# Attention in a two-layer trunk: value products turned, weights normalised ahead of their transposes

## The reference, cut to what matters

```
first layer, for each query block of 128:
  p_cmp = masked_softmax(q . k_cmp * scale)       # 15 compressed keys
  p_sel = masked_softmax(q . k_sel * scale)       # with 256 tokens all blocks are selected
  p_win = masked_softmax(q . k_win * scale)       # the window covers all tokens, causal
  o = gate0 * p_cmp @ v_cmp + gate1 * p_sel @ v_sel + gate2 * p_win @ v_win
  return o @ w_out
second layer:
  p = masked_softmax(q . k * scale); o = p @ v; return o @ w_out
masked_softmax(s) = exp(s - max) / max(sum(exp(s - max)), 1e-30)
```

## Time and profile before

| | |
|---|---|
| median of 3 runs | 763.71 us (763.39 to 764.23) |
| profiled execution | 763.77 us |
| its span | 762.0 us |
| PE busy | 717.5 us (94%) |
| DVE busy | 518.1 us (68%) |
| ACT busy | 374.0 us (49%) |
| POOL busy | 273.0 us (36%) |

### The profile page before, as it was taken

The page is one execution under the profiler, slowest core; times in us unless marked ns, Lnnn a source line. Parts: engine busy times, 40 slices in busy tenths (PEclk is TensorE's granted clock), DMA queues, the critical chain, the costliest instruction groups (busy, mean ns, idle before and its releaser), DMA issues. The chain is left out here.

```text
span 762.0 us, 11217 instructions
## 1 busy us (share of the span) xinstructions
PE 717.5 (94%) x4085; PEld 581.2 (76%) x4085; DVE 518.1 (68%) x940; ACT 374.0 (49%) x696; POOL 273.0 (36%) x261
## 2 busy tenths in 40 slices
PE   4799999889999999999999889989999999999997
PEld 2577768678687888878788777868688888878886
DVE  3357687898466796977656887987567885554544
ACT  2255555576336444444432367776356444444431
POOL 7021211000103998979969641520106960000000
PEclk9999999999999999999999999999999999999999
DMA  8997994030563888896866546801846965654521
GB/s 288 355 371 219 359 353 149 1 112 2 189 197 112 262 286 279 254 298 202 288 242 208 156 161 182 312 12 58 283 158 188 284 215 170 187 185 181 171 106 55
DMA packets 93742, 154.05 MB, mean 202 GB/s; under 512 B 6235, under 2 KB 68320, under 8 KB 93696
## 3 DMA queue, kind: packets, MB, share of 16 engines
q1 hardware_dynamic: 80768, 111.24, 44.1%
q0 software_dynamic: 12928, 42.20, 17.4%
HBM read 151.32 MB, written 1.05 MB: 200 GB/s over the span
## 5 line engine op out<-in xcount | busy, mean ns | idle before, releaser
L1079 DVE TENSOR_TENSOR w_lo<-raw,w_hi 128x1024 fp32r<-128x1024 f32 (+3 forms) x198 | 286.3, 1460 | 146.3 <-ACT w_hi L734 145.8
L734 ACT ACTIVATE w_hi<-raw 128x1024 fp32r<-128x1024 f32 (+3 forms) x198 | 201.4, 1024 | 268.8 <-PE lin L1724 244.6
L1722 PE MATMUL lin<-w_hi,st_hi 128*128 128x512 f32 (+2 forms) x568 | 227.9, 401 | 0.1
L1724 PE MATMUL lin<-w_hi,st_lo 128*128 128x512 f32 (+2 forms) x568 | 219.4, 386 | 0.0
L1723 PE MATMUL lin<-w_lo,st_hi 128*128 128x512 f32 (+2 forms) x568 | 218.8, 385 | 0.0
L602 POOL DMA_DIRECT2D ada_ring<-in_ada_w_dram x80 | 45.2, 566 | 258.5 <-PE sc L1845 221.0
L1722 PEld LDWEIGHTS lin<-w_hi,st_hi 128*128 128x128 f32 x568 | 107.5, 189 | 29.1 <-issue 8.5
L1724 PEld LDWEIGHTS lin<-w_hi,st_lo 128*128 128x128 f32 x568 | 107.4, 189 | 21.3
L1723 PEld LDWEIGHTS lin<-w_lo,st_hi 128*128 128x128 f32 x568 | 107.6, 189 | 19.0 <-issue 0.7
L681 POOL TENSOR_TENSOR pool_acc<-pool_acc,ada_ring 128x1024 f32<-128x1024 f32 x40 | 115.6, 2889 | 3.3
L1722 PE MATMUL lin<-w_hi,hid_hi 128*128 128x512 f32 x176 | 69.7, 396 | 0.4 <-DVE hid L1251 0.4
(11 more groups left out here) (262 smaller groups left out, 889.1 us busy)
## 6 DMA issues: line engine op xcount, KB each, us to landing
raw<-in_ffn_w_in_dram SPq DMA_DIRECT2D x88, 512.0 KB, 5.0
ada_ring<-in_ada_w_dram POOLq DMA_DIRECT2D x80, 512.0 KB, 4.8
raw<-in_ffn_w_out_dram SPq DMA_DIRECT2D x22, 1024.0 KB, 5.3
raw<-in_nsa_w_in_dram SPq DMA_DIRECT2D x10, 1024.0 KB, 12.6
ada_first<-in_ada_w_dram SPq DMA_DIRECT2D x8, 1024.0 KB, 13.1
raw<-in_nsa_cmp_w_dram SPq DMA_DIRECT2D x4, 1024.0 KB, 11.5
raw<-in_nsa_w_out_dram SPq DMA_DIRECT2D x4, 1024.0 KB, 9.5
raw<-in_mla_w_out_dram SPq DMA_DIRECT2D x4, 1024.0 KB, 8.2
```

The lines of the kernel that those rows point to most:

```text
L734: nc.scalar.activation(part_of(w_hi, s), raw_part(s), ACT.Copy).then_inc(hi_ready, 1)
L1079: nc.vector.tensor_tensor(part_of(w_lo, s), raw_part(s), part_of(w_hi, s).bitcast(F32), ALU.subtract).then_inc(lo_ready, 1)
L1722: nc.tensor.matmul(bank, a_h, w_h, start=first, stop=False)
L1724: return nc.tensor.matmul(bank, a_l, w_h, start=False, stop=last)
```

## The change

- Items are handled in pairs, 16 in the first layer and 8 in the second. The loops of all three engines go over pairs. A pair's scores, its transposes (two pairs later) and its value products (three pairs later) are together.
- The value products have v stationary (64 wide) and the turned weights moving; the result is the output turned (channels on partitions, tokens in columns), the two heads of a pair in the lower and upper half of the partitions. Eight items (first layer: both branches of four heads) or four (second layer) gather in one bank, so the branches of the first layer are added up by the bank. The compressed branch's product opens each bank of the first layer.
- For that the weights have to be normalised and gated before. VectorE does that: per pair, `factors` (sum times the stored 1 + exp(-gate), reciprocal) and `normalise` (four multiplications in place, 128 and 256 columns for each head). The reciprocal of the gates is gone. The compressed weights are multiplied in one operation per token tile.
- The output is evicted from its bank directly as stationary halves (`group_high` on ScalarE, `group_low` on VectorE), four groups in each layer. The transposes of the output, their evictions, and the adding into `o0` are gone.
- Of four copies to `prob_t` ScalarE now does three, VectorE one. There are six buffers for the weights and four for the turned ones.
- The banks of scores and outputs are chosen anew per layer; 12 and 6 idle products stand ahead of the two groups of compressed transposes.
- TensorE's scores wait for the maxima of two pairs before, not for exponentials.

The diff, its core (constants, declarations and bookkeeping are left out):

```diff
+T_P0 = _batches(2 * H, "act", "dve", "act", "act")
+ST_O0 = _evictions(G)
+T_P1 = _batches(H, "act", "dve", "act", "act")
+ST_O1 = _evictions(H // R)
+        score0, summed0 = [sc[0], sc[1], lin[0], lin[1]], [lin[2], lin[3]]
+        score1, summed1 = [sc[0], sc[1], lin[2], lin[3]], [lin[0], lin[1]]
 # ScalarE, attention
+                for q in range(n_pairs + 3):
+                    before(q)
+                    if q < n_pairs:
+                        for j in range(2):
+                            n = 2 * q + j
+                            act.wait_ge(maxed, item0 + n + 1)
...
+                    if q >= group + 3 and (q - 3) % group == 0 and k < groups - 1:
+                        group_high(k)
+                    for n in range(2 * q - 4, 2 * q - 2):
+                        if 0 <= n < 2 * n_pairs and TP_EMPTIED[tp0 + n] == "act":
...
 # VectorE
+            def compressed_weights(t):
+                dve.wait_ge(cmp_exped, t + 1)
+                link(nc.vector.tensor_reduce(cf, tfull[:, t, :].rearrange("p (h c) -> p h c", c=CP), X, ALU.add))
+                link(nc.vector.scalar_tensor_tensor(cf4, cf4, TINY, gates_by_pair[:, t, :, :, :, 0], ALU.max,
+                                                    ALU.mult))
+                nc.vector.reciprocal(cf, cf).then_inc(cmp_summed, 1)
+            def factors(p, item0, gated):
+                dve.wait_ge(exped, item0 + 2 * p + 2)
...
+                if gated:
+                    link(nc.vector.scalar_tensor_tensor(cf, total, TINY, gates_of(p), ALU.max, ALU.mult))
+                else:
+                    link(nc.vector.tensor_scalar(cf, total, TINY, None, ALU.max))
+                nc.vector.reciprocal(cf, cf).then_inc(factored, 1)
+            def normalise(p, pair0, prob_b):
+                dve.wait_ge(factored, pair0 + p + 1)
+                for j in range(2):
+                    buf = prob_b[(2 * p + j) % 6]
+                    for t in range(T):
+                        cols = buf[:, t * P:t * P + (t + 1) * P]
+                        ins = nc.vector.tensor_scalar(cols, cols, coef[:, p % 3, 2 * t + j:2 * t + j + 1], None, ALU.mult)
+                ins.then_inc(normed, 1)
 # VectorE, attention: scores of pair q, behind(q) = factors and normalise of pair q - 1, copies of pair q - 2, group_low
-            def nsa_step(k): ...
-            def nsa_add(k): ...
-            def output_low(batch0): ...
-            def mla_step(k): ...
 # TensorE, attention
+                def values(p):
+                    k, m = divmod(p, group)
+                    bank = banks[k % 2]
+                    if m == 0:
+                        if k >= 2:
+                            pe.wait_ge(st_ready, st0 + k - 1)
+                        bank_begun[0] = group_start(k, bank)
+                    pe.wait_ge(*emptied(tp0 + 2 * p))
+                    pe.wait_ge(*emptied(tp0 + 2 * p + 1))
+                    c0 = (p % 2) * S
+                    for t in range(T):
+                        for u in range(2):
+                            n = 2 * p + u
+                            half = slice(DH * u, DH * u + DH)
+                            ins = nc.tensor.matmul(bank[half, c0 + t * P:c0 + S], v_of(n, t),
+                                                   prob_tb[n % 4][:, t * S:t * P + S],
...
+                for q in range(n_pairs + 3):
+                    before(q)
+                    if q < n_pairs:
+                        scores(q)
+                    if 2 <= q < n_pairs + 2:
+                        pe.wait_ge(normed, pair0 + q - 1)
+                        for n in (2 * q - 4, 2 * q - 3):
+                            transposes(tp0 + n, [prob_b[n % 6][:, j * P:(j + 1) * P] for j in range(3)])
+                    if q >= 3:
+                        values(q - 3)
...
-            pe.wait_ge(o_steps, 8)
-            for m in range(2):
-                o_batch(o0)(T_O0, m)
-            unit(U_OUT0, OUT0, FOUR, 512, stationary, st_wait(T_O0, o_batch(o0)), EACH)
+            unit(U_OUT0, OUT0, FOUR, 512, stationary, output_wait(ST_O0), EACH)
```

## The result

Median 770.44 us (768.41 to 771.68, 4 runs) against 763.85 (763.39 to 764.23, 4 runs): ratio 1.0083, 95% interval 1.0057 to 1.0109. The direction was the forecast's; the size, 6.6 us for 2.8, was not, and it stands just outside 762.0 to 770.0. The profiled execution took 771.68 (span 769.9), 7.9 over that of the kernel before.

A forecast was written before the change was run, and what follows sets the result against it. TensorE was busy 94%, VectorE nearly as full in attention; after the change VectorE's queue was to bound attention. 763.8 + 1.9 + 5.9 - 3.1 - 2.2 = 766.3, with 0.2 left out by the sum 766.5 us; range 762.0 to 770.0.

The forecast's parts named there:

- Part 1: TensorE's value products in attention: a pair's two heads run side by side, 0.86 us a pair, bounds 0.7 and 1.5.
- Rival (c): Value products: the two column halves don't overlap, a pair costs 1.5 us, 771.5 us in all; chance 0.07.
- Part 2: VectorE's normalisation in attention: four multiplications in place cost 0.91 us a pair, bounds 0.68 and 1.2.
- Part 3: First layer's attention: VectorE's queue sums to 54.9 us and attention ends at 191.7, +1.9 us.
- the term of the low evictions: VectorE in the first layer's attention: three low evictions wait for ScalarE's high half, 3 x 0.6 = 1.8 us.
- Rival (a): Attention: TensorE sets the pace and is faster; 761.0 us with cheaper multiplications, 750 without VectorE waits; chance 0.14.
- Part 4: Second layer's attention: VectorE's queue sums to 34.9 us and attention ends at 536.9, +5.9 us.
- busy over 90%: Sign for both attention stages: VectorE busy over 90% between the first scores and the stage's end.
- Part 5: Boundaries behind attention: output transposes gone, the modulation chunk's transfer late next; -3.1 and -2.2 us.
- Part 6: Items priced at nothing: 18 idle products (2.0 us) and ScalarE's extra copies lie in waits or idle time.
- from the boundary on everything moves alike: Code behind the attention boundaries: POOL and SP not in the way, everything shifts together, priced at nothing.
- Rival (b): Second layer's attention: holes in TensorE's work cost it the clock, up to 1.8 us a fall, 767 to 769.5; chance 0.18.

The follow-up runs named there:

- e4: Changed kernel with one single-column multiplication in place of each pair's four normalising ones, output not the reference's; 0.9990, 763.29 us.
- e2: Kernel before with nmax grown from 32 to 48 bytes, moving the tiles behind it by 32 bytes; 1.0007.
- e5: Changed kernel with nmax made 96 bytes, putting the tiles behind it on multiples of 128 bytes; 1.0073.
- e1: Changed kernel with nmax made 64 bytes, which left all tiles at the same places, so a repeat; 1.0081.
- e3: Changed kernel with many idle products (18, 25, 10, 17) in four of TensorE's holes; 1.0155.
- e6: Changed kernel with fewer idle products (8, 10, 4, 7) in the same four TensorE holes as e3; 1.0065.
- e9: e5 with the second layer's last root sums moved to the start of its attention on VectorE; 1.0027.
- e13: Changed kernel with GpSimd leaving out its last modulation chunk, output not the reference's; 1.0061.
- e14: Changed kernel as it is, run again; 1.0087.
- e15: Changed kernel with tiles on multiples of 128 bytes, e6's idle products and GpSimd's last chunk left out; 1.0009.
- e17: Changed kernel with tiles on multiples of 128 bytes and e6's idle products, nothing left out; 1.0034.
- e16: Kernel before with GpSimd leaving out its last modulation chunk, output not the reference's; 0.9965.
- e18: Kernel before with tiles on multiples of 128 bytes, a repeat of e12; 0.9983.
- e7: e4 with ScalarE's copies of transposed weights put ahead of the exponentials of the pair two later; 0.9934.
- e10: e9 with ScalarE doing all copies of transposed weights, these and the group copies ahead of the exponentials; 0.9938.
- e12: Kernel before with nmax made 96 bytes, putting its tiles on multiples of 128 bytes; 0.9972.
- e8: e5 with the 256-column multiplications on GpSimd and the second layer's last root sums at its attention's start; 0.9995.

## Why the prediction was wrong

- **Part 1, value products**: right, 0.80 a pair (0.86 taken). Rival (c) is out.
- **Part 2, normalisation**: right, 0.93 (0.91).
- **Part 3, first layer**: +1.8 measured, +1.9 forecast, and VectorE took 55.0 for 54.9 (the term of the low evictions is 3 x 0.5 by its own working, not 3 x 0.6). The reason was half of it: e4 shows the loop through ScalarE at 2.85 a pair (3.0 with the compressed branch's share), close under VectorE's 3.2. That the forecast held without the loop is in part luck: had the multiplications been cheaper, as in e4, a sum of queues would have been far off (it promised 9.5 us for e4, and 2.5 came). Rival (a)'s 750 "if VectorE's queue gave no wait at all" overlooked this loop, which I had used for (c) only.
- **Part 4, second layer**: +5.5 without a fall in the tail (38.1 less 32.5), +5.9 forecast; VectorE took 35.0 where the sum had 34.9. The sign "busy over 90%" was met in the first layer (90%) and not in the second (82%): the sum itself had 2.9 us of waits in it, and behind VectorE's last pair TensorE works alone.
- **Part 5, boundaries**: -2.7 and -1.9 for -3.1 and -2.2; the transfer is late next, as said.
- **Part 6, at nothing**: the 18 idle products take 4.1 us and not 2.0, and were hidden even so. The words "from the boundary on everything moves alike" are the step that failed first: a term that the sum had at nothing. The tiles moved, and the down products with them: 528 x 0.0045 = 2.4 us by the rate, of which e2 and e5 find 0.5 to 1.1 in their medians.
- **Rival (b), the clock**: the step that failed second. I priced it right, 1.8 a fall for 1.6 and 1.7 measured, and then left it out of the sum, as an alternative to it, and only in the second layer. It comes on top. The holes that I named there are the ones that came (2.3 and 3.0 us for 2.4 and 3.2), but a fall behind them costs nothing; the falls that cost stand in the tail and in the first layer, which I had not named. How often they come has to be counted. The first layer has the changed kernel's order in ten traces (changed, e1, e3, e5, e6, e9, e13, e14, e15, e17), with six falls: some 1.0 us a run. The tail fell in three of the five traces with its order and without idle products (changed, e1, e5, e13, e14): 0.9 to 1.0. On the other side e2 and e16, built on the kernel before, fell at the first boundary (9.31 for 7.72 in e2), two of the five traces of that kernel and its versions: 0.6.

The Trainium skill's page TensorE: Matmul & The Clock Gate, Part 1, has the low rate as the default that recent activity lifts. The traces agree in so far as every fall in or near attention stands behind waits of TensorE: 2.21 us, ended at 144.89, in e1; 0.80 and 0.99, ended at 191.11 and 192.75, in e2. A wait does not settle it, though: e5 waited 2.20, ended at 145.27, and did not fall, nor did the kernel before behind the same two waits as e2.

So the terms of the sum make 2.7, as measured in the traces and forecast; the clock adds 1.0 + 1.0 - 0.6; the tiles add between 0.5 and 2.4. Together that is 4.6 to 6.5, for 6.6 measured. That the tiles and the clock are most of what the sum lacked is shown by e17 and e18: the kernels stand 6.6 us apart as they are, and 3.2 to 3.9 with the tiles in equal places and idle products in the holes. The split between the two is an estimate from a few traces, and up to 2 us stay open. One candidate is the norm ahead of the second layer: TensorE waited 6.1 to 6.4 us there in five of the thirteen traces of the changed kernel and its versions that have GpSimd's whole work, and 3.0 to 3.9 in all four such traces of the kernel before. The medians of e13 and e16 don't show a difference by it. The remaining +2.1 of the profiled run, at 101 us, was in one trace of the changed kernel only.

## What to carry to other kernels

After summing an engine's queue, walk the loop too: a result, its reader two stages on, and what that reader stands behind; where queue and loop are close, freeing one gives little (e4, 2.5 us) and both give more (e7, 6.4; e10, 3.9). A clock fall is an addition to the sum wherever a change opens holes, free where another engine has hardly a gap. Before comparing two versions, compare the addresses of their tiles.

## What the runs showed of the hardware that I had not expected

- The rate of 128x512 products depends on where the tile that is loaded as stationary starts: 0.227 us apart on multiples of 128 bytes, 0.229 on odd multiples of 64, 0.2333 on odd multiples of 32 (e12, before, e2). The products with `st_hi` and `st_lo`, which did not move, have a median of 0.227 in all of these.
- A 0.17 us VectorE operation can stand 2.0 us behind a GpSimd one (e14). The Trainium skill's page SBUF — State Buffer, section Who interferes with whom, states that the two share a port pair under an exclusive lock and that a tensor_scalar on VectorE can take it; the rows agree, and its neighbour at 433.65, also of that form, took 0.17; it started while GpSimd was between two instructions. Larger ones are held up too: VectorE's 128x576 subtraction took 2.93 beside GpSimd's addition and 0.76 without it (before, e16), and in e8 the second 128-column multiplication of a pair 0.51 for 0.28.
